# A hybrid attention layer on one core: weight sums loaded by GpSimd's queue, and no steps of the sums in units 110 to 119

## The reference

```python
def conv_ffn(h, w_up, conv_w, conv_b, w_down):
    u = h @ w_up                                   # 2048 x 11264
    up = jnp.pad(u, ((0, 0), (CONV_WIDTH - 1, 0), (0, 0)))
    u = sum(conv_w[j] * up[:, j:j + S] for j in range(CONV_WIDTH)) + conv_b
    a, b = jnp.split(u, 2, axis=-1)
    return (jax.nn.silu(a) * b) @ w_down           # 5632 x 2048
...
    p = h @ w_in[l]                                # input projection, then attention and recurrence
    x = x + mix @ w_out[l]
    h = rms_norm(x, ffn_norm[l])
    x = x + conv_ffn(h, w_ffn_up[l], ffn_conv_w[l], ffn_conv_b[l], w_ffn_down[l])
```

## Time and profile before

| | |
|---|---|
| median of three runs | 1083.93 us (1083.36 to 1084.04) |
| the profiled execution, and its span | 1085.06 us, span 1083.2 us |
| PE busy | 1074.6 us (99%) |
| DVE busy | 907.2 us (84%) |
| ACT busy | 638.1 us (59%) |
| POOL busy | 87.5 us (8%) |
| chain that ended last | PE 95%, DMA 3%, DVE 1% |
| DMA, mean over the span | 253 GB/s |

### The profile page before, as it was taken

The page is one execution under the profiler, slowest core; times in us unless marked ns, Lnnn a source line. Parts: engine busy times, 40 slices in busy tenths (PEclk is TensorE's granted clock), DMA queues, the critical chain, the costliest instruction groups (busy, mean ns, idle before and its releaser), DMA issues.

```text
span 1083.2 us, 18131 instructions
## 1 busy us (share of the span) xinstructions
PE 1074.6 (99%) x6537; PEld 925.9 (85%) x6537; DVE 907.2 (84%) x1342; ACT 638.1 (59%) x934; POOL 87.5 (8%) x130
## 2 busy tenths in 40 slices
PE   9999999999999999999999999999999999999998
PEld 8888888888888888888888888888888887787887
DVE  7888988979655578888888889888887888998998
ACT  7677675757445555555555555545554566657763
POOL 4500000000010010100100010001010000000000
PEclk9999999999999999999999999999999999999999
DMA  8656679787799988988988988989988689989794
GB/s 277 180 170 193 182 234 243 228 242 225 255 246 281 274 249 251 260 259 254 262 240 257 265 253 265 250 238 293 280 253 236 196 296 308 326 295 340 269 339 154
DMA packets 197008, 274.00 MB, mean 253 GB/s; under 512 B 9285, under 2 KB 144086, under 8 KB 196694
## 3 DMA queue, kind: packets, MB, share of 16 engines
q1 hardware_dynamic: 180758, 220.69, 62.4%
q0 software_dynamic: 12960, 47.19, 20.0%
q10 hardware_dynamic: 3232, 5.39, 1.3%
HBM read 267.86 MB, written 52.56 MB: 296 GB/s over the span
## 4 chain that ended last, share of the span: by engine, by line
PE 95%; DMA 3%; DVE 1%; issue 0%; ACT 0%; SPq 0%; DVEq 0%; ACTq 0%
PE bank L1828 38%; PE bank L1836 20%; PE bank L2221 6%; PE bank L2223 6%; PE bank L2222 6%; PE bank L2074 3%; PE bank L2075 3%; PE bank L2076 3%; PE bank L1875 2%; PE bank L1877 2%; PE bank L1876 2%; DMA slot<-u_sums 1%; PE bank L1796 1%; PE bank L1904 1%; DMA raw<-in_w_ffn_up_dram 1%; DMA xt<-in_x_dram 1%
## 5 line engine op out<-in xcount | busy, mean ns | idle before, releaser
L796 ACT CAST w_hi<-raw 128x1024 fp32r<-128x1024 f32 x299 | 312.3, 1049 | 245.9 <-PE bank L1836 107.3
L1209 DVE TENSOR_TENSOR w_lo<-raw,w_hi 128x1024 fp32r<-128x1024 f32 x299 | 364.0, 1222 | 107.2 <-ACT w_hi L796 106.5
L1828 PE MATMUL bank<-hs,w_hi 128*128 128x512 f32 x1792 | 423.0, 391 | 0.0
L1828 PEld LDWEIGHTS bank<-hs,w_hi 128*128 128x128 f32 x1792 | 331.2, 188 | 66.3 <-issue 0.9
L1836 PEld LDWEIGHTS bank<-hs,w_lo 128*128 128x128 f32 x1792 | 224.6, 191 | 5.7 <-issue 0.2
L1836 PE MATMUL bank<-hs,w_lo 128*128 128x256 f32 x1792 | 227.3, 283 | 0.0
L1175 ACT CAST hi_slot<-slot 128x1024 fp32r<-128x1024 f32 (+1 forms) x108 | 124.3, 1187 | 65.4 <-PE bank L2223 19.1
L1736 DVE TENSOR_TENSOR slot_lo<-slot,hi_slot 128x1536 fp32r<-128x1536 f32 (+1 forms) x74 | 142.1, 1957 | 3.6 <-ACT hi_slot L1175 2.4
L1654 DVE SCALAR_TENSOR_TENSOR C<-U,cols,C 128x256 f32<-128x256 f32 x176 | 73.4, 479 | 0.0
L2223 PE MATMUL bank<-hi_slot,gated 128*128 128x512 f32 (+1 forms) x186 | 72.0, 387 | 0.0
L2221 PE MATMUL bank<-hi_slot,gated 128*128 128x512 f32 (+1 forms) x186 | 72.0, 387 | 0.0
(11 more groups left out here) (249 smaller groups left out, 1191.2 us busy)
## 6 DMA issues: line engine op xcount, KB each, us to landing
raw<-in_w_ffn_up_dram SPq DMA_DIRECT2D x176, 512.0 KB, 5.7
u_sums<-in_w_ffn_down_dram POOLq DMA_DIRECT2D x62, 512.0 KB, 6.1
raw<-in_w_in_dram SPq DMA_DIRECT2D x51, 512.0 KB, 4.5
slot<-in_w_ffn_down_dram SPq DMA_DIRECT2D x40, 512.0 KB, 5.0
raw<-in_w_in_dram SPq DMA_DIRECT2D x66, 256.0 KB, 3.6
slot<-u_sums SPq DMA_DIRECT2D x22, 768.0 KB, 5.9
raw<-in_w_out_dram SPq DMA_DIRECT2D x32, 512.0 KB, 5.8
u_sums<-u_sums POOLq DMA_DIRECT2D x28, 512.0 KB, 7.2
```

The costliest lines, as they stand in the source:

```text
L796: act.copy(w_hi[:, i, :], raw[:, i, :]).then_inc(units_hi, 1)
L1209: dve.tensor_tensor(w_lo[:, i, :], raw[:, i, :], w_hi[:, i, :].bitcast(F32), ALU.subtract)\
L1828: m = pe.matmul(banks[b][:, :], w_hi[:, i, c], hs[:, 4 * i + k, :], start=(first and k == 0), stop=(final and k == 3))
```

## The change

Two things. The loads of the sums in Down move from SP's queue to GpSimd's. GpSimd waits until all up units are used and all steps have landed, and then, for each seven, waits until the slot's y blocks are used and loads the first two sums; where the fourth sum comes from DRAM, it waits until the z blocks are used and loads it by a DMA of its own with a semaphore of its own, for which ACT waits ahead of its copy of z. SP no longer waits for the steps, nor for y and z.

And the steps come every 8/3 units in place of every 14/5, and a second pause lies over units 110 to 119. The waits for the first use of a slot are written in another way (`last_old_in`).

```diff
-SUM_STEP = (14, 5)
-FIRST_SUM_UNIT, SUM_PAUSE = 20, (30, 38)
+SUM_STEP = (8, 3)
+FIRST_SUM_UNIT, SUM_PAUSES = 20, [(30, 38), (110, 120)]
...
+        fourth_loaded = [sem(f"fourth_loaded{n}") for n in range(SMALL_SLOT)]
...
+        def fourth_sums_loaded(q):
+            n = sum(last_sum_in_dram(m) and SLOT_OF[m] == SLOT_OF[q] for m in range(OLD_RING, q + 1))
+            return 16 * n
...
+        def last_old_in(units):
+
+            return max(n for n in range(LAST_OLD - RING + 1, LAST_OLD + 1) if n % RING in units)
...
+        def wait_for_slot(engine, q, part):
+
+            before = raw_part_before(q, part)
+            if before is not None:
+                wait_until_used(engine, before)
+            elif SLOT_OF[q] == 2:
+                wait_until_used(engine, last_old_in({"a": (0, 1), "x": (0, 1), "y": (1, 2), "z": (2,), "b": (2, 3)}[part]))
+            elif SLOT_OF[q] == SMALL_SLOT and part == "b":
+                wait_until_used(engine, last_old_in((3,)))
...
-                wait_for_slot(q, "x")
+                wait_for_slot(sp, q, "x")
                 sp.dma_start(raw_blocks[:, 0:2, :], w_down_v[:, 2 * n + 1, :, pair, :]).then_inc(first, 16)
                 sp.dma_start(raw_blocks[:, 2, :], w_down_v[:, 2 * n, 1, pair, :]).then_inc(first, 16)
-                wait_for_slot(q, "y")
-                sums = 2
-                if last_sum_in_dram(q):
-                    wait_for_slot(q, "z")
-                    sums = 3
-                sp.dma_start(raw_blocks[:, 3:3 + sums, :],
-                             u_sums_v[n, 0:sums, :, pair, :].rearrange("j p m -> p j m")).then_inc(others, 16)
...
-            sp.wait_ge(sums_added, 16 * (2 * SEVENS + len(LAST_SUM_IN_DRAM)))
...
-                if unit >= SUM_PAUSE[0]:
-                    unit += SUM_PAUSE[1] - SUM_PAUSE[0]
+                for first, end in SUM_PAUSES:
+                    if unit >= first:
+                        unit += end - first
...
+            def load_sums(pair, at):
+
+                q, n = q_of(pair, at), K_PAIR_AT[pair][at]
+                others = loaded_of(q, "b")
+                raw_blocks = slots[SLOT_OF[q]][0]
+                wait_for_slot(pool, q, "y")
+                pool.dma_start(raw_blocks[:, 3:5, :],
+                             u_sums_v[n, 0:2, :, pair, :].rearrange("j p m -> p j m")).then_inc(others, 16)
+                if last_sum_in_dram(q):
+                    wait_for_slot(pool, q, "z")
+                    pool.dma_start(raw_blocks[:, SUM_4_AT, :], u_sums_v[n, 2, :, pair, :])\
+                        .then_inc(fourth_loaded[SLOT_OF[q]], 16)
+
+            wait_until_used(pool, Q_DOWN * RING - 1)
+            pool.wait_ge(sums_added, 16 * added)
+            for pair in range(COLUMN_PAIRS):
+                for at in SEVEN_AT[pair]:
+                    load_sums(pair, at)
...
                     if part == "z":
                         act.wait_ge(sums_of_block_made, seven_of(pair, at) + 1)
+                        if last_sum_in_dram(q):
+                            act.wait_ge(fourth_loaded[SLOT_OF[q]], fourth_sums_loaded(q))
```

More of the change, by code:

```diff
@@ L645, in load_old @@
                         .then_inc(loaded[unit % RING], 16)
[L647 to L655, removed]
             def load_seven(pair, at):
                 q, n = q_of(pair, at), K_PAIR_AT[pair][at]
-                first, others = loaded_of(q, "a"), loaded_of(q, "b")
+                first = loaded_of(q, "a")
                 raw_blocks = slots[SLOT_OF[q]][0]
-                wait_for_slot(q, "x")
+                wait_for_slot(sp, q, "x")
                 sp.dma_start(raw_blocks[:, 0:2, :], w_down_v[:, 2 * n + 1, :, pair, :]).then_inc(first, 16)
                 sp.dma_start(raw_blocks[:, 2, :], w_down_v[:, 2 * n, 1, pair, :]).then_inc(first, 16)
-                wait_for_slot(q, "y")
-                sums = 2
-                if last_sum_in_dram(q):
-                    wait_for_slot(q, "z")
-                    sums = 3
-                sp.dma_start(raw_blocks[:, 3:3 + sums, :],
-                             u_sums_v[n, 0:sums, :, pair, :].rearrange("j p m -> p j m")).then_inc(others, 16)
             def load_four(pair, at):
@@ L676, in load_four @@
                 for r, piece in enumerate("ab"):
-                    wait_for_slot(q, piece)
+                    wait_for_slot(sp, q, piece)
                     sp.dma_start(raw_of(q, piece), w_down_v[:, 2 * K_PAIR_AT[pair][at] + r, :, pair, :])\
@@ L1165, in hi_of @@
                         act.wait_ge(sums_of_block_made, seven_of(pair, at) + 1)
+                        if last_sum_in_dram(q):
+                            act.wait_ge(fourth_loaded[SLOT_OF[q]], fourth_sums_loaded(q))
                     else:
                         wait_for_down(act, q, {"x": "a", "y": "b"}.get(part, part))
[L1168 to L1172, removed]
+                    first_use = q < OLD_RING + HI_SLOTS
+                    if first_use and q % HI_SLOTS == 0:
+                        of_raw = last_old_in({"x": (0, 1), "y": (1, 2), "z": (2, 3)}[part])
+                        act.wait_ge(units_split, of_raw + 1 + RING)
+                    elif first_use:
+                        if part == "x":
+                            act.wait_ge(units_split, last_old_in((3,)) + 1 + RING)
+                        wait_until_used(act, last_old_in({"x": (0,), "y": (1,), "z": (2,)}[part]))
                     else:
@@ L1749, in sums_of_weights @@
                 elif SLOT_OF[q] == 2:
-                    wait_until_used(dve, LAST_OLD)
+                    wait_until_used(dve, last_old_in((2, 3)))
                 if not last_sum_in_dram(q):
```

## The result

The changed kernel took 1086.08 us (median of 15 runs, 1085.09 to 1089.65) beside 1083.53 us for the kernel before (15 runs, 1081.71 to 1084.63): a ratio of 1.0029, with a 95% interval of 1.0021 to 1.0037. It is slower. (The two medians alone give 1.0024; the ratio and its interval are taken from all runs.) The forecast was 1079.0 with a range of 1077.8 to 1084.3.

The account below looks back on a forecast made before the run. PE's own waits were taken as the bound: 1.47 us at the end of the projection plus 3.5 of 4.5 us lost in Down gave 5.0 us off, 1079.0 us for the median, range 1077.8 to 1084.3.

Parts of the forecast that it names:

- place one: End of the output projection, near 370 us: PE's 1.47 us wait for xt, forecast to go with the second pause.
- The budget of the sums: Down: sums land in 6.7 us, inside budgets of 7.8 and 8.4 us by 1.1 and 1.7 us.
- The two long stalls: Down: PE's two waits for DVE's split, 1.7 us in all, behind late sums loads; both forecast to go.
- SP gains nothing: Down: SP's dropped waits change nothing, as the next x loads behind them wait for a later event anyway.
- The fourth: Down: fourth sum loaded by itself behind z on GpSimd, with 1.6 us of room and no new stall.
- Rival 1: Down stays as x loads share the DMA engines with the sums; only place one won, 1082.5 us; chance 0.15.
- Rival 3: GpSimd's sums land late in general, paid once in three sevens, 11.3 times; slower, for instance 1092.6 us; chance 0.10.
- Rival 4: GpSimd's DMA descriptors wait for DVE in Down, a load coming to 8.6 us; 1091.4 us; chance 0.04.
- What stays: Down: 1.0 of the 4.5 us lost was left, put down to DVE running behind PE.

Follow-up runs that it names:

- e1_pause_only: The changed kernel's new timetable of steps alone, sums still loaded by SP as in the kernel before; 1082.76 us, 0.9999 to the kernel before.
- e2_gpsimd_only: The changed kernel with the old timetable of steps, so only the sums' move to GpSimd; 1086.76 us, 1.0032 to the kernel before.
- e10: Changed kernel with the fourth sum back on SP, which waits for z only where a fourth is loaded; 1085.21 us, 1.0013 to the kernel before.
- e9a: Changed kernel with the fourth sum back on SP, which waits for z at every seven; 1082.16 us, 0.9991 to the kernel before.
- e6: Changed kernel, all sums on GpSimd, but SP waits for z behind every seven's x part; 1084.52 us, 1.0013 to the kernel before.
- e9b_fourth_gpsimd: Changed kernel with the two sums back on SP behind y, only the fourth on GpSimd; 1083.62 us, 1.0005 to the kernel before.
- e3_split_on_sp: Changed kernel with the sums still split in two loads but all issued by SP behind the x part; 1081.67 us, 0.9984 to the kernel before.
- e17_mirror: Changed kernel with queues exchanged: sums on SP, Down's other loads behind the first units on GpSimd; 1085.68 us, 1.0029 to the kernel before.
- e16: e3_split_on_sp with all of Down's loads behind the first units issued by GpSimd, same order; 1105.83 us, 1.0203 to the kernel before.
- e5: Changed kernel, but SP waits for y, and z where a fourth is loaded, as before; 1085.77 us, 1.0024 to the kernel before.

## Why the prediction was wrong

The sign was wrong: 5.0 us less were forecast, some 3 us more were measured. About 1.5 us of the miss lie in place one, the rest in Down.

**Place one, 1.47 us of the sum.** The stall is gone in after, as forecast, and so far the reading of the earlier trace rows stands: with no step across them the loads land in a median of 4.6 us (4.5 in e1_pause_only). The failed step is the size. The stall was taken as one of every execution, but it was 0.3 us in another one of the same kernel and absent in e2_gpsimd_only, which has the same timetable, although the loads there took medians of 8.3 and 7.6 us: late loads need not reach PE. The pause alone gives 0.9999 (0.9991 to 1.0008), so less than 1 us. The hint stood in the prediction itself: the profiled execution lay 1.1 us above the median, and the sum subtracted from the median a stall that the faster profile hardly has. The same holds for 1.5 of the 4.5 us lost in Down.

**The budget of the sums, 1.1 and 1.7 us of room.** The taken time to landing was nearly right as a median: 6.7 us forecast with 0.3 us of reaction, 0.39 + 6.6 us measured (GpSimd's own instruction in it, put at 0.84 us, takes 0.71). The two long stalls of before did go: the sums of those sevens, issued at 907.07 and 987.66 in after, land after 7.1 and 6.5 us, and PE doesn't stop there. The failed step is that one middle time was held against the budget for all 34 loads, though those of the earlier trace rows reached 9.1 us: what lies past 7.8 or 8.4 us is paid, and what lands early gives nothing back. Five loads, issued at 935.75, 982.90, 998.33, 1034.34 and 1054.10, landed after 7.5 to 8.9 us, and these are the five new stalls. Ahead of each, by up to 0.7 us, SP had issued x2, the parked sums or the eights' loads. That isn't the whole of it: x2 went out ahead at 925.66 and 1043.35 too, and the sums there took 6.5 and 6.6 us. The trace also has the sixteen semaphore increments that make up a landing. For 982.90, 998.33 and 1054.10 the ninth came after 7.3 to 7.6 us, where its median is 5.5, so the whole load was late; for 935.75 and 1034.34, beside x2 alone, it came after 6.0 and 6.1 us, and only the last few were late, which the order doesn't explain by itself.

**"SP gains nothing" from its dropped waits.** This is one of the two steps that cost most. It looked at the next x loads alone, which do wait for a later event. At other turns the parked sums, the eights' loads and x2 stand behind the same waits, and they went out with the x part, ahead of GpSimd's sums. Holding them back again is worth 0.0022 (e10 to e9a), or 0.0016 with the fourth on GpSimd (changed kernel to e6, intervals that overlap).

**The fourth, "1.6 us of room, no new stall".** No engine waits for line 796 in after, so the fourth was in time, as forecast. It was too early: in e9b_fourth_gpsimd it lands ahead of loads that were issued before it and are needed sooner. Its move costs 0.0022 (e9a to e6), as much as SP's dropped waits; the prediction put it at nothing.

**Rival 1** had the mechanism, x loads and sums that share the DMA engines instead of queueing, but let it cost at most the gain; its price below nothing was missing. On one queue the split in two loads gains 0.0016 (e3_split_on_sp, with the new timetable, which alone gives 0.9999), on two it loses 0.0029: 0.0045 for the second queue and the waits that go with it. The Trainium skill has the rule that the prediction should have weighed as a rival (DMA: Bandwidth & Descriptors, section "Queues, rings and completion order"): each DMA engine takes turns between the queues that have work for it, a packet at a time. The landings above agree with it in that a load on the other queue delays the sums, 6.0 against 8.7 us for the same load; that the turns are by packets isn't seen here.

**Rival 3**, sums of GpSimd that land late in general, gave the right sign from the wrong cause. It priced lateness at every third seven, 11.3 times; it was five stalls of 4.4 us in all, at the loads just named, and Down loses as much in e17_mirror, 7.7 us, with the sums on SP. **Rival 4** isn't seen: GpSimd's DMA instructions in Down last 704 to 776 and 557 to 578 ns, while DVE is busy 63.41 of 70 us from 980 to 1050. The waits for DVE that it needs would spread them.

**What stays**, taken at 1.0 us and put down to DVE, is about 2: Down loses 2.0 us in e9a_two_sums_gpsimd with no wait of PE in Down that its view lists. That these are DVE's isn't shown.

What stays open: whether GpSimd's queue costs something of its own where the order is kept. The 0.0007 from e3 to e9a are within the intervals, and e16, meant for it, met what looks like a limit on loads at once. And what delays single parts of a load, as in turn 3 of e6_sp_waits_z_always.

## What to carry to other kernels

A queue is a priority list: moving one kind of load to a second queue puts it beside everything the first queue has issued and will issue, so before the move go through each turn and name what is then carried out beside the load that is needed first, and what stood behind the waits that move away. A load that hangs on too late an event can be split in two on the same queue, which keeps the order; with the new timetable this gave 0.9984 here (1081.7 us, e3_split_on_sp). Hold the slowest loads, not the median, against a budget that has to be kept at every turn. And before a stall enters a sum, look for it in a second profile: the 1.5 and 1.7 us that this prediction was made of were 0.3 and 0.5 us in the next execution.

## What the runs showed of the hardware that was not expected

- GpSimd issues a load 0.39 us after PE's event (997.94 in after), SP 0.07 us after it (908.98 to 909.05).
- GpSimd's queue stopped issuing with four loads, 1.75 MB, on their way, until 0.3 us after the second had landed: 3.5 us at 917.2 in e16_all_on_gpsimd, and 42.7 us before one line. All 25 waits of this kind over 1.5 us there end 0.31 to 0.35 us after a landing.
- The same load of 512 KB, the sums of turn 6 in the second half, took 6.0 and 7.3 us with 1 MB on another queue issued from 1 us behind it (e9a, e6), and 8.7, 8.8 and 9.0 us where the first half of that went out 0.4 to 0.7 us ahead of it (e10, changed kernel, e5). At turn 3, beside the parked sums, it took 6.9 and 8.0 us against 8.0, 7.9 and 8.0 us in the same runs.
- A load issued 1.36 us later behind the same backlog was used at nearly the same moment (5.97 us after its issue for 7.26, and 6.15 for 7.80).
